# Moving 64 key-row products and 16 value rounds of one tile to later stages, and laying weights and states out contiguously, in an RWKV-7 + GLA step with PEER experts

## The reference, cut to what matters

```python
for li in range(2):
    mod = silu(c) @ ada_w[li] + ada_b[li]              # six vectors of 1024
    hm = rmsnorm(x, norm1_g[li]) * (1 + sc1) + sh1
    out, S = rwkv7_mix(hm, ...) if li == 0 else gla_mix(hm, ...)
    x = x + gt1 * out
    hc = rmsnorm(x, norm2_g[li]) * (1 + sc2) + sh2
    q = (hc @ peer_wq[li]).reshape(n, 8, 2, 128)       # queries
    s = einsum('thpk,hpnk->thpn', q, subkeys)          # scores
    # top 16 of each half, the 256 sums, top 16 of those: expert ids, gate = softmax
    act = gelu(einsum('thed,td->the', u[expert], hc))  # key rows
    x = x + gt2 * einsum('the,thed->td', gate * act, v[expert])  # value rows
y = rmsnorm(x, final_g)
```

## Time and profile before

| | |
|---|---|
| three runs | 2929.86, 2939.84, 2946.71 us; median 2939.84 |
| the profiled execution | 2938.69 us, its span 2936.6 us |
| granted TensorE clock, mean of the span | 0.802 |
| busy: PE, DVE, POOL, ACT | 66%, 54%, 45%, 10% |
| chain that ended last, by engine | PE 31%, DVE 25%, DMA 21%, POOL 11%, issue 7%, ACT 3% |
| moved by DMA | 840.72 MB, mean 286 GB/s |

### The profile page before, as it was taken

How to read it: one execution, slowest core, us unless ns; L and a number is a source line. 1 busy time by engine, 2 the same in 40 slices (tenths; PEclk the granted TensorE clock), 3 DMA queues, 4 the chain that set the end, 5 groups by cost and what they waited for, 6 DMA issues and landing times.

```text
span 2936.6 us, 26684 instructions
## 1 busy us (share of the span) xinstructions
PE 1934.3 (66%) x10129; PEld 1224.6 (42%) x10129; DVE 1594.2 (54%) x2987; ACT 280.3 (10%) x442; POOL 1315.3 (45%) x1160
## 2 busy tenths in 40 slices
PE   6889857938868776567667758678247864453533
PEld 2379613427836335354245227363125433350100
DVE  5253386574933646768312147875961738766033
ACT  1111000111100010000100110001100000000000
POOL 0000013442643655656334235556754675467774
PEclk8889979967879887677789879789578986676876
DMA  7520687963789896767998869789888998899997
GB/s 262 206 97 1 212 301 254 327 230 121 250 277 330 306 339 212 254 208 250 341 343 331 308 241 335 265 301 398 292 280 342 407 386 296 277 355 385 409 410 311
DMA packets 303193, 840.72 MB, mean 286 GB/s; under 512 B 46030, under 2 KB 57214, under 8 KB 303068
## 3 DMA queue, kind: packets, MB, share of 16 engines
q0 software_dynamic: 165888, 604.05, 56.5%
q1 hardware_dynamic: 126612, 230.60, 22.2%
q10 hardware_dynamic: 10568, 4.38, 0.6%
HBM read 828.63 MB, written 10.31 MB: 286 GB/s over the span
## 4 chain that ended last, share of the span: by engine, by line
PE 31%; DVE 25%; DMA 21%; POOL 11%; issue 7%; ACT 3%; PEld 1%; SPq 0%; ACTq 0%; DVEq 0%; PEldq 0%; POOLq 0%
PE psum L1939 29%; DVE arena L1126 9%; POOL arena L720 8%; DVE arena L1106 7%; DMA arena<-in_peer_v,idx_v 7%; POOL wring L720 2%; DMA wring<-in_peer_wq 2%; DMA wring<-in_ada_w 2%; DMA wring<-in_gla_w_in 2%; DMA wring<-in_rw_w_rkv 2%; DMA out<-arena 1%; DVE hT L1106 1%; PE psum L1957 1%; DMA hc<-in_peer_v,idx_v 1%; DMA wring<-in_peer_v,idx_u 1%
## 5 line engine op out<-in xcount | busy, mean ns | idle before, releaser
L720 POOL DMA_INDIRECT arena<-in_peer_u,idx_u x560 | 730.3, 1304 | 1058.8 <-DVE acts L1126 498.8
L1939 PE MATMUL psum<-arena 128*32 128x512 f32 (+6 forms) x3662 | 622.0, 569 | 436.9 <-DMA arena<-in_peer_v,idx_v 170.9
L1126 DVE CUSTOM_DVE_ANT_0 arena<-arena,hc 128x1024 f32<-128x1024 f32 x544 | 644.3, 1224 | 83.6 <-DMA arena<-in_peer_u,idx_u 57.1
L720 POOL DMA_INDIRECT arena<-in_peer_v,idx_v x428 | 424.2, 991 | 463.4 <-PE psum L1939 341.4
L1939 PEld LDWEIGHTS psum<-arena 128*32 128x32 f32 (+2 forms) x3662 | 325.0, 171 | 659.5 <-issue 467.1
L1939 PE MATMUL psum<-pick,ident 128*128 128x256 f32 x1038 | 263.5, 409 | 47.2 <-DVEq L1385 37.7
L1939 PE MATMUL psum<-wring,arena 128*32 128x512 f32 (+3 forms) x728 | 216.3, 677 | 79.4 <-DMA wring<-in_peer_v,idx_v 42.4
L1939 PEld LDWEIGHTS psum<-pick,ident 128*128 128x128 f32 x1038 | 206.3, 204 | 134.9 <-issue 57.0
L1939 PE MATMUL psum<-hT,wring 128*128 128x128 f32 (+3 forms) x1824 | 238.0, 293 | 23.3 <-DMA wring<-in_peer_wq 13.6
L1939 PEld LDWEIGHTS psum<-hT,wring 128*128 128x128 f32 (+1 forms) x1824 | 225.8, 198 | 46.3 <-issue 21.3
L1939 PE MATMUL psum<-wring,hT 128*128 128x512 f32 (+1 forms) x480 | 192.4, 560 | 14.5 <-DMA wring<-in_gla_w_in 10.9
(11 more groups left out here) (234 smaller groups left out, 1785.8 us busy)
## 6 DMA issues: line engine op xcount, KB each, us to landing
wring<-in_ada_w SPq DMA_DIRECT2D x24, 2048.0 KB
wring<-in_peer_wq SPq DMA_DIRECT2D x24, 2048.0 KB
wring<-in_rw_w_rkv SPq DMA_DIRECT2D x12, 2048.0 KB
wring<-in_gla_w_in SPq DMA_DIRECT2D x12, 2048.0 KB
wring<-in_rw_wo SPq DMA_DIRECT2D x6, 2048.0 KB
wring<-in_gla_wo SPq DMA_DIRECT2D x6, 2048.0 KB
vring<-mod_d SPq DMA_DIRECT2D x20, 512.0 KB
arena<-in_peer_u,idx_u POOLq DMA_INDIRECT x560, 6.2
```

The costliest lines, as they stand in the source:

```text
L720: pool.indirect_dma_start(slot(s, n), None, v_rows if side else u_rows, bass.IndirectOffsetOnAxis(index, 0)).then_inc(rows_landed[s], 16)
L1126: dve.tensor_tensor_reduce(slot(s, n), slot(s, n), hidden(li, t), 1.0, 0.0, MUL, ADD, acts[:, (3 * li + t) % 2, col:col + 1]).then_inc(row ...
L1939: return nc.tensor.matmul(out, lhsT, rhs, start=start, stop=stop)
```

## The change

Six things are edited.

1. In core(S) the rate of the key products of (0,1) is halved, and only the first 64 of them are opened; their gelu, `weigh` and `build` come at the end of the second half of core(S) only.
2. The other 64 key products of (0,1) are opened in out(0,S), after the second norms, in 16s ahead of each of the four score fills. Their weights follow there, and the 32 value rounds of (0,1) begin at the end of out(0,S). Before, 16 rounds stood at the end of core(S) and in out(0,S), and 16 in gla_mixer(0).
3. Of these 32 rounds 16 now stand in gla_mixer(0) as before, 3 in its tail, and 13 in out(1,0): four after the output projection, one each at three places ahead of the queries, six among the queries. `add_experts(0,1)` moves from the end of gla_mixer(0) to out(1,0), behind the search of the best keys of the first half.
4. The 32 key products of (0,S) stood among the steps of out(1,0) at a rate of 7. They now stand in one block behind `add_experts(0,1)`.
5. SP loads the modulation row for that `add_experts` after the output weights and keys of out(1,0).
6. The host lays out all weights, the keys and the RWKV and GLA states so that each load and store reads one contiguous run for a partition: 16 KB for a weight load, where it was 8 runs of 2 KB.

```diff
-                cols = src.shape[1]
-                sp.dma_start(wring[:, b, :, 0:cols], src.rearrange("(k p) n -> p k n", p=P)).then_inc(weight_loaded[b], 16)
+                cols = src.shape[1] // KD
+                sp.dma_start(wring[:, b, :, 0:cols], src.rearrange("p (k n) -> p k n", k=KD)).then_inc(weight_loaded[b], 16)
...
             vec(row("gla_gnorm"))
+            out_weights(a["gla_wo"])
+            gla_out(0)
             mod_vec(0, 5)
-            out_weights(a["gla_wo"][0])
-            gla_out(0)
...
-            RATES = {"mix": 14, "core1": 1.9, "core2": 4.0, "enter": 6, "gla": 2.6, "out": 7}
+            RATES = {"mix": 14, "core1": 1.9, "core2": 2.0, "query": 16, "enter": 6, "gla": 2.6, "out": 7}
...
-                    weights_due(0, 1, hh)
-                    if hh == 0:
-                        open_rows(0, 1, 64, 64, RATES["core2"])
+                    if hh:
+                        weights_due(0, 1, 0)
...
-                else:
-                    add_experts(0, 1, add_tmp)
...
-                if li and t == 0:
-                    open_rows(0, SAMPLE, 0, SHORT, RATES["out"])
...
                     adaln((0,))
+                    open_rows(0, 1, 64, 64, RATES["query"], True)
...
-                    if li and t < SAMPLE and half == 0:
-                        weights_due(*((0, SAMPLE), (1, 0, 1))[t])
+                    if li and t == 0 and half == 0:
+                        add_experts(0, 1, add_tmp)
+                        open_rows(0, SAMPLE, 0, SHORT, 0)
+                        weights_due(0, SAMPLE)
+                    if li and t == 1 and half == 0:
+                        weights_due(1, 0, 1)
...
-                    fan_weights(0, 1, hh)
-                if sample:
-                    open_values(0, 1, VALUE_RATES["out"])
+                    if hh:
+                        fan_weights(0, 1, 0)
...
-                if tiles[0]:
-                    rounds_now(4 if li else 1)
+                rounds_now({(0, 1): 1, (1, 0): 4, (1, 1): 4}.get((li, tiles[0]), 0))
...
-                        rounds_now({(0, SAMPLE): 1, (1, 1): 2}.get((li, tiles[0]), 0))
+                        rounds_now({(1, 0): 1, (1, 1): 2}.get((li, tiles[0]), 0))
...
+                if li == 0 and tiles[0] == SAMPLE:
+                    fan_weights(0, 1, 1)
+                    open_values(0, 1, VALUE_RATES["out"])
                 if li and tiles[0] == 0:
+                    rest_values()
                     open_values(0, SAMPLE, 0)
...
+    def tiled(w, n=512):
+        v = w.reshape(w.shape[:-2] + (KD, P, w.shape[-1] // n, n))
+        v = np.moveaxis(v, -2, -4)
+        v = np.swapaxes(v, -3, -2)
+        return v.reshape(v.shape[:-2] + (KD * n,))
```

More of the change, by code:

```diff
@@ L493, in ada @@
                 for j in range(2 * k, 2 * k + 2):
-                    parts_buffer[li, k] = weight(a["ada_w"][li][:, j * 512:(j + 1) * 512])
+                    parts_buffer[li, k] = weight(a["ada_w"][li, j])
             def mod_rows(li, k):
@@ L509, in lora_inputs @@
             def lora_inputs():
-                for src, lo in ((a["rw_w1"], 0), (a["rw_a1"], 64), (a["rw_g1"], 128)):
-                    cols = src.shape[2]
-                    sp.dma_start(lora1[:, :, lo:lo + cols], src[0].rearrange("(k p) n -> p k n", p=P)).then_inc(lora_loaded, 16)
+                sp.dma_start(lora1, a["lora1"].rearrange("p (k n) -> p k n", k=KD)).then_inc(lora_loaded, 16)
             def rkv(i, halves=(0, 1)):
                 for j in halves:
-                    weight(a["rw_w_rkv"][0, i][:, j * 512:(j + 1) * 512])
+                    weight(a["rw_w_rkv"][0, i, j])
             def head_vecs():
@@ L524, in keys @@
                 sp.wait_ge(region_free, w.next(region_free))
[L525 removed]
+                sp.dma_start(sk[:, :, :], a["peer_subkeys"][li].rearrange("n (i k) -> n i k", i=HP)).then_inc(keys_loaded, 16)
             def queries(li):
                 for j in range(4):
[L529 removed]
+                    weight(a["peer_wq"][li, j])
             def out_weights(src):
                 for j in range(2):
[L533 removed]
+                    weight(src[j])
             def gla_weights(blocks):
                 for j in blocks:
[L537 removed]
+                    weight(a["gla_w_in"][j] if j < 6 else a["gla_w_low"])
             def gla_gate_weights(tiles):
@@ L2519, in _ @@
             sum_lanes()
-_INS = ["x_prompt", "x_sample", "state_rwkv_S", "state_rwkv_shift", "state_gla_S", "c_prompt", "c_sample",
-        "ada_w", "ada_b", "norm1_g", "norm2_g", "final_g",
-        "rw_mu", "rw_w_rkv", "rw_w0", "rw_w1", "rw_w2", "rw_a0", "rw_a1", "rw_a2", "rw_g1", "rw_g2",
-        "rw_kk", "rw_ka", "rw_rk", "rw_lnx_w", "rw_lnx_b", "rw_wo",
-        "gla_w_in", "gla_wa2", "gla_ba", "gla_gnorm", "gla_wo",
-        "peer_wq", "peer_subkeys", "peer_u", "peer_v"]
+_INS = ["x_prompt", "x_sample", "state_rwkv_shift", "c_prompt", "c_sample",
+        "ada_b", "norm1_g", "norm2_g", "final_g",
+        "rw_mu", "rw_w0", "rw_w2", "rw_a0", "rw_a2", "rw_g2",
+        "rw_kk", "rw_ka", "rw_rk", "rw_lnx_w", "rw_lnx_b",
+        "gla_wa2", "gla_ba", "gla_gnorm", "peer_u", "peer_v"]
 _OUTS = [(1, 256, 1024), (8, 4, 1024), (1, 1, 16, 64, 64), (1, 1, 1024), (1, 1, 4, 128, 256),
-         (1, 8, 16, 64, 64), (1, 8, 1024), (1, 8, 4, 128, 256)]
+         (DEC_B, 2, RK, HALF_H * RK), (1, 8, 1024), (GH, GK, DEC_B * GV)]
 def kernel(**inputs):
@@ L2535 @@
     from concourse.bass_utils import run_bass_kernel_spmd
+    def tiled(w, n=512):
[3 more added lines that the diff above has]
+        return v.reshape(v.shape[:-2] + (KD * n,))
+    laid = {name: inputs[name] for name in _INS}
+    for name in ("ada_w", "rw_w_rkv", "peer_wq"):
+        laid[name] = tiled(inputs[name])
+    for name in ("rw_wo", "gla_wo"):
+        laid[name] = tiled(inputs[name][0])
+    laid["gla_w_in"] = tiled(inputs["gla_w_in"][0][:, 0:3072])
+    laid["gla_w_low"] = tiled(inputs["gla_w_in"][0][:, 3072:3088], 16)[0]
+    laid["lora1"] = tiled(np.concatenate([inputs[name][0] for name in ("rw_w1", "rw_a1", "rw_g1")], axis=1), 256)[0]
+    keys = inputs["peer_subkeys"]
+    laid["peer_subkeys"] = keys.transpose(0, 3, 1, 2, 4).reshape(2, NKEYS, HP * keys.shape[4])
+    laid["state_rwkv_S"] = inputs["state_rwkv_S"].reshape(DEC_B, 2, HALF_H, RK, RK).transpose(0, 1, 3, 2, 4).reshape(DEC_B, 2, RK, HALF_H * RK)
+    laid["state_gla_S"] = inputs["state_gla_S"][0].transpose(1, 2, 0, 3).reshape(GH, GK, DEC_B * GV)
     nc = bacc.Bacc("TRN2", target_bir_lowering=False, num_devices=1)
     arrays, aps = {}, {}
-    for name in _INS:
-        v = np.ascontiguousarray(inputs[name])
+    for name, v in laid.items():
+        v = np.ascontiguousarray(v)
         arrays["in_" + name] = v
@@ L2545 @@
     r = run_bass_kernel_spmd(nc, [arrays], core_ids=[0])
-    return tuple(r.results[0][f"out_{i}"] for i in range(len(_OUTS)))
+    y_p, y_s, S_p, sh_p, G_p, S_s, sh_s, G_s = (r.results[0][f"out_{i}"] for i in range(len(_OUTS)))
+    S_s = S_s.reshape(DEC_B, 2, RK, HALF_H, RK).transpose(0, 1, 3, 2, 4).reshape(1, DEC_B, RH, RK, RK)
+    G_s = G_s.reshape(GH, GK, DEC_B, GV).transpose(2, 0, 1, 3)[None]
+    return (y_p, y_s, S_p, sh_p, G_p, np.ascontiguousarray(S_s), sh_s, np.ascontiguousarray(G_s))
```

36 lines of the change are left out of this document (15 added, 21 removed).

## The result

The changed kernel is slower by about 1%: median 2962.78 us of six runs (2959.62 to 2986.09), against 2938.01 us before (six runs, 2928.85 to 2946.71). The ratio is 1.0101, with a 95% interval of 1.006 to 1.0141. The forecast was 2901 us, faster, in a range of 2830 to 2960.

What follows compares the result with a forecast made beforehand. No single bound: DVE ends last in core(S), DMA is nearly full in out(0,S)'s queries, only gathers remain from 2667. Terms -65 - 9 + 11 + 0 + 72 - 47 = -38 against 2938.69 gave 2901 us, range 2830 to 2960.

Steps and rivals of the forecast that it cites:

- The order's terms: Core(S), out(0,S) ahead of the queries, its queries, gla_mixer(0) and out(1,0): -65, -9, +11, 0 and +72 us.
- the -27 for weight waits in the later stages: Part of the weights' term: gla_mixer(1,S) -9, out(1,1) query load -9, out(0,1) -4, other out(1,0..1) and state transfers -5.
- core(S) and the norms: Core(S) -65 us, mainly halved products (-49) and shorter state waits (-14); out(0,S) ahead of the queries -9.
- The queries: Queries of out(0,S): 64 added products wait for gathers, 117 us for 106, +11; bounds -5 and +25.
- gla_mixer(0): Gla weight arriving sooner, -7, against added tail rounds, +7: 0 us; bounds -12 and +15.
- out(1,0): 13 rounds at 6.85 us, then addition and 32 products ahead of gelu: +72 us; bounds +45 and +100.
- Weights elsewhere: Contiguous loads beside gathers take 11.2 us, not about 20.9, so PE waits less: -47 us; bounds 0 and -75.
- (C): Rival: contiguous loads no faster beside gathers; weights -5, schedule +9, time 2938 to 2945; chance 0.14.
- three signs of being wrong: Core(S) keeps 290 us or more; total ready before first half's best keys; loads still take 18 us or more.
- Rival (A): Later stages hide more: out(1,0) only +20, time 2849, or 2830 with core(S)'s lower bound; chance 0.15.
- Rival (B): Out(1,0) one serial chain, +100, core(S) only -45: 2982, if total(0,1) comes later than about 1905; chance 0.17.
- (D): Rival: loads land in 7 us, weights -60, but starved gathers give +20 back: 2905; chance 0.54 together with the forecast.

Runs made afterwards that it cites:

- second profile: The profile of run e8, the changed kernel run once more, unaltered; 2960.65 us.
- e1: The layout alone: the changed kernel with all edits of the order undone; 2898.36 us, ratio 0.9875 to the kernel before.
- e8: The changed kernel run again, unaltered, for a second profile nearer the median than the first; 2960.65 us.
- e2: The order alone: the changed kernel with weights, lora, keys and states in the old pieces; 2998.4 us, ratio 1.0197 to the kernel before.
- e9: The changed kernel with ten weight loads cut to an eighth (queries of out(0,S) and out(1,0), first two GLA loads); 2941.51 us, ratio 1.0026.
- e5: The kernel before, in its order, with only the weight loads contiguous; 2912.2 us, ratio 0.9912.
- e6: The kernel before, in its order, with only lora weights, keys and states contiguous; 2930.78 us, ratio 0.9975.
- e3: The changed kernel with the 16 moved value rounds back in gla_mixer(0), addition and (0,S) products as before the change; 2959.46 us, ratio 1.0086.
- e4: The changed kernel with the second 64 key products of (0,1) opened earlier, at the end of core(S); 2933.51 us, ratio 0.9988.

## Why the prediction was wrong

Two steps failed. The order's terms (+9 together) left out what the ring does while a stage changes and PE's own work between the rounds: the order alone measured +60. And the -27 for weight waits in the later stages gave nothing (+0.5), because gathers were late next there. By the prediction's own steps, against the second profile:

- **core(S) and the norms: right in the sum, partly by luck.** -65 and -9 were forecast, -77.3 measured. The chain of the second profile by line, 1063 to 1316:

```profile
by line: PE psum L1933 30.7%; DVE arena L1102 14.4%; DVE arena L1122 10.6%; ACT arena L762 7.1%; DMA hT<-in_state_rwkv_S 5.8%; DVE hT L1102 4.8%; issue 4.7%; PE psum L2260 4.6%; DMA out<-arena 3.4%; DMA wring<-in_ada_w 3.1%; PE psum L2207 2
```

  Of 253 us the products are 27, where the earlier trace rows has 98 of 315; state loads and stores are 23, where they were 45. So the products gave -71 where -49 was forecast and the state waits -22 for -14, while PE's main line on the chain grew from 30 us (9.6%) to 78 (30.7%), for which the sum had no term.
- **The queries: +11 forecast, +27.7 measured**, beyond the bound of +25. The length itself was nearly right: 117 us and 43 MB were forecast, 122.1 us measured, and the 123 us window at 352 GB/s moved 43.3 MB. Wrong was what it was taken from: the 106 us are the window up to 1586, but the last copy stood 94.4 us behind the first query load. And products could not start before the norm, so that the ring had its eight rows and no more, however long POOL had waited.
- **gla_mixer(0): 0 forecast, +7.9 measured.** e1 shows that the layout gave its -10.8 there; the order alone cost +8.5 (187.5, e2; 184.4 and 186.7 in the first profile and e9).
- **out(1,0): +72 forecast, +87.6 measured.** The path was right: the total was expected 116 us into the stage and came at 131.4; the block was priced at 40 and took 40.4. But a round took 9.0 us, not 6.85 and 11 over all. The prediction let the queries' matmuls lie in the ring's waits and had no term for the 36 matmuls on `pick`. On the chain both stand between the rounds, and a gather follows only behind them:

```profile
1723.27 19.51 PE psum L1933 x101
1743.04 0.94 POOL arena L716
...
1752.89 13.86 PE psum L1933 x93
...
1802.92 13.72 PE psum L1933 x101
```

  In these pieces the `pick` row takes 15.81 us and two blocks of query matmuls 8.44 and 7.31 (at 1756.46 and 1807.49). Without them 85.0 of the 116.6 us are left, by this estimate 6.5 a round, near the ring's 6.85. That is read from the chain; no run tested it.
- **Weights elsewhere: -47 forecast, -24.0 measured.** At the start -14.0 (forecast -7) and in mix(1,S) -10.5 (-13) the sum is near, in part by luck: up to the end of mix(1,S) e5 wins 15.6 us and e6 9.2, so by these profiles more than a third is the small tensors', for which the sum had nothing there. The -27 for out(0,1), gla_mixer(1,S), out(1,1) and the rest became +0.5: -1.6 and +2.1. By stages this is the largest miss. The step that failed counted each load's wait on the chain as gain and did not ask, as it did for PE in mix(1,S), what would be late next: gathers, as the two chains under e1 show. It was not the loads' length: by the packets of the second profile, the 34 of its 84 loads of 2 MB with more than 0.5 MB of gathers beside them took 7.5 us in the median (6.3 to 10.3), less than the 11.2 of the sum. That the whole layout is still worth 40 us comes also from core(S) and gla_mixer(0), where the sum had part of it in other terms (-14 and -7), so its nearness to -47 is luck too. And there it does not add to the order's gain: core(S) with the norms is -19.1 by the layout alone, -67.6 by the order alone, -77.3 by both.

By halves, each run alone, most of the miss is the order's: the terms other than the weights' were +9 (as (C) has it), and the order alone is 60 us slower than before (e2, medians); the layout's -47 was -40 (e1).

Four of five terms erred to the same side, 60 us in all: 17 + 8 + 16 + 23, less 3. What the order's terms have in common e2, e3 and e4 show: products and rounds were priced by what DVE and the chain lose or save in the stage where they stand, not by what the ring does meanwhile. Half of the key rows taken out of core(S) left POOL standing for 84.71 us; every value row of (0,1) is behind them in POOL's order, and their gathers began at 1391.0 before and at 1493.2 in the second profile, though the query loads had begun 103 us earlier in it than before (1376.5 and 1479.9).

None of the prediction's three signs of being wrong came: core(S) took 253 us and not 290, the addition still waited for PE (1.81 us), and loads took 7.5 us and not 18. The signs watched the path, and the miss is in the sizes and in work that was given no time.

Rival (A) fails, as out(1,0) gave +87.6 and not +20. Rival (B) named the slower outcome (0.17) and its place, but not its condition: core(S) gave more than expected, and the total came at 1753 + 131 = 1884 on the scale of before, not after 1905. Rival (C) is refuted by e1 for the whole, though no gain is what the stages behind gla_mixer(0) show. Of (D), the loads are about as short as it said (7.5 us for 7), and they do hold gathers back in the queries (e9: 13.7 us); but its price was taken as a case near the forecast instead of being put into the sum (by its own terms it comes to 2908, not 2905). By the Trainium skill (DMA: Bandwidth & Descriptors, section SWDGE vs HWDGE vs iDMA), where it describes the descriptors that GpSimd builds, packets of at most 4096 B are preferred. The long runs that SP loads were not cut to that size here: q1's mean packet is 8.0 KB.

What stays open: with an eighth of the query loads (e9) a round in out(1,0) still takes 8.2 us (13 from 1689.53 to 1795.76), where the ring gave 6.85 in gla_mixer(0). The chain has PE's own matmuls between the rounds, and no run took them away. Nor does a run show what sets the stages behind gla_mixer(0) once the loads are short; the chain of e1 names gathers. The kernel that beats both is e1, 1.25% under the kernel before.

## What to carry to other kernels

When several consumers draw on one ring in a fixed order, price a move by the ring: ask how long the producer stands still after it, and which work is behind that in its order. A wait that a faster load removes is worth what is late next in that stage, so look at the chain for the second latest before adding such waits up. And where a change has two independent parts, run each alone: here one was worth -40 us and the other +60, where the sum had -47 and +9.

## What the runs showed of the hardware

A load's time beside gathers went with the length of its runs: with runs of 2 KB against rows of 4 KB PE waited 6.84 and 4.40 us for a block's weights in mix(1,S), with runs of 16 KB not at all (0.30 and 0.45 us between blocks), while the rows' queue carried the same bytes. On the chain such a load stood for 18 to 21 us before (18.46 at 527.43, 20.90 in the earlier trace rows); with long runs such loads took 7.5 us in the median from the first packet to the last. Without gathers the longer runs won little: a load on the chain at the start took 7.75 us, and 7.58 us in the first profile of the changed kernel. And POOL's issue of a gather took 0.94 us in one place and 1.68 us where DVE had just begun a row of products (1391.12 above); what sets the longer one was not tried.
